# A transformer's first mixer: buffers, batches and order of the convolution's taps on three engines

## The reference

```python
a, gate = split(u)                      # 512 channels each
h = a * sigmoid(gate)
h = depthwise_causal_conv(h, conv_dw)   # 31 taps per channel
h = silu(layer_norm(h + conv_dw_b)) @ w_conv_pw
attn = sliding_window_attention(q, k, v, sinks, rel_bias)   # window 128
x = x + rms_norm(concat(attn, h) @ w_out)
```

## Time and profile before

| | us |
|---|---|
| median of 3 runs | 2300.67 (2300.66 to 2301.5) |
| the profiled execution | 2300.79 |
| its span, first to last instruction | 2299.0 |
| TensorE busy | 2266.1 (99%) |
| VectorE busy | 1358.1 (59%) |
| ScalarE busy | 1037.4 (45%) |
| GpSimd busy | 1028.4 (45%) |
| mean granted TensorE clock | 0.997 of full speed |

### The profile page before, as it was taken

How to read it: one execution, slowest core, us unless ns; L and a number is a source line. 1 busy time by engine, 2 the same in 40 slices (tenths; PEclk the granted TensorE clock), 3 DMA queues, 4 the chain that set the end, 5 groups by cost and what they waited for, 6 DMA issues and landing times.

```text
span 2299.0 us, 30705 instructions
## 1 busy us (share of the span) xinstructions
PE 2266.1 (99%) x11442; PEld 1889.6 (82%) x11442; DVE 1358.1 (59%) x2182; ACT 1037.4 (45%) x2057; POOL 1028.4 (45%) x900
## 2 busy tenths in 40 slices
PE   9989999999999999999999999999999999999998
PEld 7777788888888888888898878887888888888887
DVE  6996516954545477775633775154594444547776
ACT  6577735433232345455634765135443323234543
POOL 2886535488787700032112031224448878770003
PEclk9999999999999999999999999999999999999999
DMA  6122134233233368664002001243223323336865
GB/s 213 37 74 79 51 123 134 73 110 126 85 125 104 113 247 297 213 208 127 20 10 72 24 10 38 76 163 110 101 78 102 126 85 126 103 116 247 295 211 194
DMA packets 218980, 278.48 MB, mean 121 GB/s; under 512 B 16396, under 2 KB 142988, under 8 KB 215760
## 3 DMA queue, kind: packets, MB, share of 16 engines
q1 hardware_dynamic: 199056, 212.81, 29.3%
q10 hardware_dynamic: 19776, 63.71, 7.0%
HBM read 208.30 MB, written 68.17 MB: 120 GB/s over the span
## 4 chain that ended last, share of the span: by engine, by line
PE 87%; POOL 4%; DVE 3%; ACT 3%; issue 1%; DMA 1%; SPq 0%; POOLq 0%; ACTq 0%; DVEq 0%
PE P L513 25%; PE P L515 25%; PE P L514 25%; POOL acc L1315 3%; PE P L3242 3%; PE P L3261 2%; PE P L3277 2%; PE P L3199 1%; PE P L525 1%; ACT wh L473 1%; PE P L1602 1%; DVE P L1242 0%; DVE P L1235 0%; PE P L809 0%; PE P L1627 0%
## 5 line engine op out<-in xcount | busy, mean ns | idle before, releaser
L513 PE MATMUL P<-ah,wh 128*128 128x512 f32 x1120 | 440.6, 393 | 8.4 <-DVE wl L479 4.8
L515 PE MATMUL P<-ah,wl 128*128 128x512 f32 x1120 | 437.6, 391 | 0.0
L514 PE MATMUL P<-al,wh 128*128 128x512 f32 x1120 | 437.1, 390 | 0.0
L513 PE MATMUL P<-wh,ah 128*128 128x512 f32 (+2 forms) x1128 | 425.9, 378 | 0.0
L515 PE MATMUL P<-wh,al 128*128 128x512 f32 (+2 forms) x1128 | 423.3, 375 | 0.0
L514 PE MATMUL P<-wl,ah 128*128 128x512 f32 (+2 forms) x1128 | 422.9, 375 | 0.0
L595 POOL TENSOR_TENSOR stats<-stats,epsc 128x1 f32<-128x1 f32 x70 | 27.7, 396 | 633.0 <-ACT xn L2088 421.0
L513 PEld LDWEIGHTS P<-ah,wh 128*128 128x128 f32 x1120 | 211.3, 189 | 54.6 <-issue 6.9
L515 PEld LDWEIGHTS P<-ah,wl 128*128 128x128 f32 x1120 | 210.9, 188 | 44.3
L514 PEld LDWEIGHTS P<-al,wh 128*128 128x128 f32 x1120 | 211.3, 189 | 43.0
L515 PEld LDWEIGHTS P<-wh,al 128*128 128x128 f32 x1128 | 212.2, 188 | 36.9
(11 more groups left out here) (399 smaller groups left out, 4433.2 us busy)
## 6 DMA issues: line engine op xcount, KB each, us to landing
rf<-ff_rows SPq DMA_DIRECT2D x154, 256.0 KB, 5.3
stage<-in_w_down_dram SPq DMA_DIRECT2D x110, 256.0 KB, 3.8
ff_rows<-sb ACTq DMA_DIRECT2D x22, 1024.0 KB, 5.0
stage<-in_w_gu_dram SPq DMA_DIRECT2D x44, 512.0 KB, 5.1
stage<-in_w_gate_dram SPq DMA_DIRECT2D x22, 512.0 KB, 4.1
stage<-in_w_up_dram SPq DMA_DIRECT2D x22, 512.0 KB, 5.1
ff_rows<-uo ACTq DMA_DIRECT2D x22, 512.0 KB, 3.0
stage<-in_w_down_dram SPq DMA_DIRECT2D x22, 512.0 KB, 5.1
```

What stands on the lines that cost most here:

```text
L513: e.matmul(out, lh, rh, start=start, stop=False, skip_group_check=onto)
L514: e.matmul(out, lh, rl, start=False, stop=False, skip_group_check=onto)
L515: return e.matmul(out, ll, rh, start=False, stop=stop, skip_group_check=onto)
```

## The change

There are now four product places of 512 columns, in the same memory; a half product takes one, a wide one two, and a wide product waits for the addition two before it, the first two wide ones for the last half. VectorE's 19 taps of block 2 end in a tile of their own, `taps_of_2`, where the sigmoid buffers were. ScalarE's product of tap 19 starts `acc` of block 2, the other eleven are added without waiting for VectorE, and a new last addition of GpSimd adds `taps_of_2`. All that waited for the last tap waits for this. The batches of products behind the th = 1 copies have 3 instead of 4. VectorE does 7 of the 14 taps behind `glu(0, 1)` and the lower half of piece 5, and the lower halves of pieces 7 and 9 move ahead of the last 7 taps and of `glu(c, 1)`.

```diff
--- before.py
+++ after.py
@@ -990,7 +990,8 @@
     acc_split = acc[:, :, :].rearrange("p c (two n) -> p c two n", two=2)
     SPLIT = (1, 3)
     tap_sums = sb("tap_sums", [128, 4, 16], off["extra"])
-    tap_products = [sb(f"tap_product{i}", [128, 1024], off["extra"] + 256 + 4 * KB * i) for i in range(2)]
+    taps_of_2 = sb("taps_of_2", [128, 1024], off["sg"])
+    tap_products = sb("tap_products", [128, 4, 512], off["extra"] + 256)
     roots = sb("token_roots", [128, 1024], off["extra"] + 256 + 8 * KB)
 
     def first_piece(port, part, landing, key):
@@ -1224,7 +1225,7 @@
                 ins = e.tensor_scalar(both, hp[:, c, 0:1024], cwt[:, c, 0:1], bias, ALU.mult, ALU.add)
             else:
                 behind("whole")
-                ins = e.scalar_tensor_tensor(acc[:, c, :] if j == SHARED - 1 else both, hp[:, c, j:j + 1024],
+                ins = e.scalar_tensor_tensor(taps_of_2[:, :] if j == SHARED - 1 else both, hp[:, c, j:j + 1024],
                                              cwt[:, c, j:j + 1], both, ALU.mult, ALU.add)
         elif name == "even":
             w = cwt[:, c, 2 * j:2 * j + 1]
@@ -1276,9 +1277,23 @@
 
     PRODUCTS = [(0, a, a + 512, w) for a in (0, 512) for w in range(TAPS)]
     PRODUCTS += [(2, 0, 1024, w) for w in range(SHARED, TAPS)]
-    STARTS = {(0, 0, 0), (0, 512, 0)}
+    STARTS = {(0, 0, 0), (0, 512, 0), (2, 0, SHARED)}
     ADDED = [(c, a, b, w) for c, a, b, w in PRODUCTS if (c, a, w) not in STARTS]
+    HALVES = sum(b - a == 512 for _, a, b, _ in ADDED)
     ADDED_AT = {(c, a, w): k for k, (c, a, b, w) in enumerate(ADDED)}
+
+    def product_place(k):
+
+        c, a, b, w = ADDED[k]
+        if b - a == 512:
+            return tap_products[:, k % 4, :]
+        return tap_products[:, 2 * (k % 2):2 * (k % 2) + 2, :].rearrange("p i n -> p (i n)")
+
+    def place_left(k):
+
+        if k < HALVES:
+            return k - 4
+        return k - 2 if k >= HALVES + 2 else HALVES - 1
 
     def some_products(n):
 
@@ -1291,28 +1306,29 @@
                     AC.wait_ge(ev, ("u", c, th))
                 AC.wait_ge(l_misc, "all")
                 AC.wait_ge(zf, "hp")
-                e.activation(acc[:, c, a:b], src, ACT.Identity, bias=cwt[:, c, 31:32], scale=weight).then_inc(
-                    *ep.up((c, a, w)))
+                if c:
+                    ins = e.activation(acc[:, c, a:b], src, ACT.Copy, scale=weight)
+                else:
+                    ins = e.activation(acc[:, c, a:b], src, ACT.Identity, bias=cwt[:, c, 31:32], scale=weight)
+                ins.then_inc(*ep.up((c, a, w)))
             else:
                 k = ADDED_AT[c, a, w]
                 for th in range(b // 512):
                     AC.wait_ge(ev, ("u", c, th))
-                if k >= 2:
-                    c2, a2, _, w2 = ADDED[k - 2]
+                if place_left(k) >= 0:
+                    c2, a2, _, w2 = ADDED[place_left(k)]
                     AC.wait_ge(pt, (c2, a2, w2))
-                e.activation(tap_products[k % 2][:, 0:b - a], src, ACT.Copy, scale=weight).then_inc(*ep.up((c, a, w)))
+                e.activation(product_place(k), src, ACT.Copy, scale=weight).then_inc(*ep.up((c, a, w)))
             n -= (b - a) / 512
 
     def pool_taps(c):
         for k, (c_, a, b, w) in enumerate(ADDED):
             if c_ == c:
                 PL.wait_ge(ep, (c, a, w))
-                if c:
-                    PL.wait_ge(tap, ("whole", 2, SHARED - 1))
                 if k:
                     c2, a2, _, w2 = ADDED[k - 1]
                     PL.wait_ge(pt, (c2, a2, w2))
-                PL.e.tensor_tensor(acc[:, c, a:b], acc[:, c, a:b], tap_products[k % 2][:, 0:b - a], ALU.add).then_inc(
+                PL.e.tensor_tensor(acc[:, c, a:b], acc[:, c, a:b], product_place(k), ALU.add).then_inc(
                     *pt.up((c, a, w)))
 
     def mixer1_act():
@@ -1391,7 +1407,7 @@
                 kv_copy(name, th)
                 if th == 0:
                     send_to(c + i + 3)
-                some_products(4)
+                some_products(3 if th else 4)
             if name == "q0":
                 for g in range(2):
                     AC.wait_ge(tp, ("v1", g))
@@ -1479,10 +1495,11 @@
         glu(1, 1)
         low_by_dve_to(4)
         add_taps(1)
-        some_taps(14)
+        some_taps(7)
         glu(0, 1)
         low_by_dve_to(5)
         DV.ends("u0")
+        some_taps(7)
         for c in range(2, 4):
             some_taps(9)
             gate(c)
@@ -1490,9 +1507,10 @@
             some_taps(5)
             values(c)
             glu(c, 0)
-            some_taps(12)
+            some_taps(5)
+            low_by_dve_to(2 * c + 3)
+            some_taps(7)
             glu(c, 1)
-            low_by_dve_to(2 * c + 3)
             add_taps(c)
         low_by_dve_to(first["kvq"])
         for i, name in enumerate(KVQ):
@@ -1516,6 +1534,9 @@
         PL.wait_ge(pz, "kp1")
         pool_taps(0)
         pool_taps(2)
+        PL.wait_ge(tap, ("whole", 2, SHARED - 1))
+        PL.wait_ge(pt, (2, 0, TAPS - 1))
+        PL.e.tensor_tensor(acc[:, 2, :], acc[:, 2, :], taps_of_2[:, :], ALU.add).then_inc(*pt.up((2, "whole")))
         PL.ends("q3")
 
 
@@ -1640,7 +1661,7 @@
             b = SWA_BANK["yc", tb]
             claim(b, cp, ("yc", tb))
             for c in range(4):
-                PE.wait_ge(*((tap, ("out", c, 0)) if c in SPLIT else (pt, (2, 0, TAPS - 1))))
+                PE.wait_ge(*((tap, ("out", c, 0)) if c in SPLIT else (pt, (2, "whole"))))
             for c in range(4):
                 ins = e.transpose(P[:, b, 128 * c:128 * c + 128], conv_rows(c, tb), ident[:, :])
             ins.then_inc(*tp.up(("yc", tb)))
@@ -1798,7 +1819,7 @@
             DV.wait_ge(nb, "b1")
             DV.wait_ge(sm, "nsink")
             if i in (2, 3):
-                DV.wait_ge(pt, (2, 0, TAPS - 1))
+                DV.wait_ge(pt, (2, "whole"))
             if i >= 4:
                 DV.wait_ge(tp, ("swa", i - 4))
             elif i < 2:
@@ -1874,7 +1895,7 @@
             PL.e.tensor_tensor(p, p, swa_rows(n)[2][:, 2 * g:2 * g + 2].unsqueeze(2).to_broadcast([128, 2, W]),
                                ALU.mult).then_inc(*nr.up(("swa", i)))
 
-        PL.wait_ge(pt, (2, 0, TAPS - 1))
+        PL.wait_ge(pt, (2, "whole"))
         for i in range(2):
             sink_column(i)
         for i in range(N1 + 4):
```

## The result

The changed kernel takes **2306.03 us** (median of 11 runs, 2305.65 to 2306.99) against 2300.78 for the kernel before (11 runs): a ratio of 1.0023, 95% interval 1.0015 to 1.0031. It is slower by 5.2 us. The profiled execution took 2306.6, with a span of 2304.8 against 2299.0, 5.8 more.

The account below looks back on a forecast made before the run. GpSimd's last addition was taken to set the start of attention. 2300.79 less 0.4 for its earlier end plus 1.9 for TensorE's slow clock gave 2302.3 for the profiled run, 2302.2 for the median; range 2298.0 to 2305.5.

Parts of the forecast that it names:

- the new waits at 143 to 157: GpSimd's waits for products late in the convolution, forecast at 1 to 2 us each.
- +1.9 forecast: At the start of attention: TensorE's clock falls after a longer idle, costing 2.4 less 0.5 of later slack.
- Last addition: 146.5 + 32.0 + 2.5 = 181.0: GpSimd's third block: first wide addition at 146.5, twelve taking 32.0, waits 2.5; the end 0.4 earlier than 181.40.
- Bounds: the same lower half took 1.23 and 1.70 ..., about 2 us, either way: Uncertainty from lower halves lengthening beside GpSimd's additions: half of some ten times 0.47 in the stage, about 2 us.
- VectorE is 0.8 later at the sigmoid of block 2: After the moved taps VectorE waits 1.7 for TensorE, to 57.6, and everything behind that sigmoid is 0.8 later too.
- that gives the 0.8 back and VectorE is level from 95.85: At piece 8 VectorE waits 1.65 instead of 2.65 because ScalarE is no longer late, recovering the 0.8.
- gains of 3.0 and 0.2: GpSimd: 3.0 from its next addition coming at 121.1, 0.2 from no longer waiting for VectorE's last tap.
- 1.5, 1.2 and 1.1: GpSimd's new waits: 1.5 at the last half product, 1.2 at the first wide product, and 1.1 more.
- C: Rival, 13%: TensorE's clock stays low through the first attention steps, 183.3 to 195, losing 5.5; time 2305.0.
- D: Rival, 22%: the clock does not fall in the idle ahead of attention, or added waits just balance; time 2300.3.
- B: Rival, 12%: GpSimd keeps ahead without new waits, VectorE's queue is next; 4.6 at most, 2296.1, likelier half 2298.4.
- A: Rival, 3%: TensorE bounds the first stage, so its stalls count in full, 11.3 us; time 2289.4.

Follow-up runs that it names:

- e10: Changed kernel with the lower half of piece 14 made three taps earlier, while GpSimd waits: 2302.95 us, ratio 1.0010.
- e15: Kernel before with the lower half of piece 14 made three taps later, beside wide additions: 2304.49 us, ratio 1.0014.
- e1: Changed kernel with VectorE doing 14 taps again, not 7, ahead of the second product of block 0: 2303.57 us, ratio 1.0011.
- e14: Changed kernel with 14 taps again ahead of the product of block 0 and piece 14's lower half three taps earlier: 2300.64 us, ratio 0.9997.
- e5: Kernel before with only the four product places and the rule for them: 2298.05 us, ratio 0.9987.
- e12: Kernel before with the four product places and ScalarE's copies of v ahead of its copies of q0: 2299.67 us, ratio 0.9995.
- e2: Changed kernel with batches of 4 products again behind every copy, not 3 behind the upper-token ones: 2306.42 us, ratio 1.0021.
- e6: Changed kernel with both 14 taps ahead of the product of block 0 and batches of 4 again: 2303.18 us, ratio 1.0009.
- e7: Kernel before with only the own place for VectorE's third-block taps, tap 19 starting ScalarE's sum, and GpSimd's last addition: 2302.19 us, ratio 1.0007.
- e8: Kernel before with only the lower halves of pieces 7 and 9 made 7 taps earlier: 2303.37 us, ratio 1.0012.

## Why the prediction was wrong

**Right.** GpSimd's last addition set the start of attention, in both kernels: the first transposes follow it by 2.26 and 2.27. The removed stalls of TensorE were worth nothing. VectorE waits at 57 (2.17; forecast 1.7), GpSimd's wait near 122 is 1.77 (1.3), the new waits at 143 to 157 are there. TensorE's clock fell, at +1.9 forecast and 1.5 to 2.3 measured. With GpSimd's end put right (3.8 later in place of 0.4 earlier) the forecast's own sum gives 2306.5 for the profiled execution, which took 2306.6. That closeness is partly chance, as the clock's term is known to 0.8 only.

**Wrong.** The failed step is "Last addition: 146.5 + 32.0 + 2.5 = 181.0", with its term "Bounds: the same lower half took 1.23 and 1.70 ..., about 2 us, either way". I kept each lower half at its old length at its new place. It depends on what GpSimd does at that moment: e10 shows 1.21 against 3.41 for the same piece, e15 3.01 against 1.21. GpSimd ended at 185.19, 4.2 later than forecast: the first wide addition was 2.05 late (148.55 for 146.5), and the wait ahead of 171.97 was 2.70, not 0.5. That wait is piece 14 and the sum of rows ahead of it, 3.4 longer on VectorE; e10 takes it away and GpSimd ends 3.1 earlier. The upper end of the range fell short by 0.5 us.

The lateness of the first wide addition comes from the step before: "VectorE is 0.8 later at the sigmoid of block 2" and "that gives the 0.8 back and VectorE is level from 95.85". It was 1.57 late at 72.93 and still 1.51 late at 97.36. The moved taps were given their wait for TensorE (2.17 for 1.7), but not the 0.83 by which piece 5 is longer at its new place, and piece 7 takes 0.80 more as well. e1 undoes the wait and piece 5 and is worth 3.0 at GpSimd's end. With both undone (e14) the end is 6.1 earlier and the time is that of the kernel before. The two terms come to more than the 3.8 by which the changed kernel is late, because its other parts, the four places above all, gain.

Two sums in the prediction do not hold as written, without weight for the result. The "gains of 3.0 and 0.2" less "1.5, 1.2 and 1.1" are 0.6 later, not 0.4 earlier; what is missing is the wait of 1.16 that the old kernel had ahead of GpSimd's run at 131.47, and which the longer run of 14 halves removes. And the estimate from the Trainium skill's 426.7 and 215.7 ns ("TensorE: Matmul & The Clock Gate", Wait — 56ns, not 53.3ns?) is 2.5, not 2.6: ten times 0.211, and 0.4 for the transposes. The trace's own spacings, 0.43 and 0.227, are near it.

Of the rivals, C came out with the right sign and near the right time by a reason that was not the one: the slow clock cost 1.5 to 2.3, not 5.5, and the rest was GpSimd's end. D is refuted by the granted clock of 0.50 in 184 to 192. B is what four places do without the change's other parts: e5 has it, at 2298.05 (B's likelier half: 2298.4), though there TensorE comes last and not VectorE, so the agreement is luck. A, TensorE as the bound, is refuted by the changed kernel, where TensorE reached the scores 2.1 earlier (177.79 for 179.91) and the end came later, and by e12, where it reached them 9 us earlier than in e5 and nothing was gained (VectorE's last conversion was 2.9 later there).

The Trainium skill ("SBUF — State Buffer", Who interferes with whom) says that a VectorE instruction with two SBUF inputs contends with a GpSimd instruction that reads SBUF, and calls the port pair that they share an exclusive lock. As an estimate from that rule and the rows here, a lower half that comes just behind the start of a wide addition (2.4) waits for up to all of it and takes up to about 3.6 with its own 1.2. The trace agrees: the longest single lower halves beside wide additions took 3.01 to 3.43, others there 1.67 to 2.45, and the taps, with one input in PSUM, kept their 0.75. What the runs show by themselves is that the length hangs on GpSimd's work beside it; that the port is the reason is the Trainium skill's. The bound that I should have used is, for every such operation, one whole addition.

Left open: the split of e2's lost gain between piece 13 and the order of products was not tried by itself, nor was the changed kernel without the place of its own for VectorE's taps. Nor was e5 with its copies of v moved only behind the q0 products, which might shorten TensorE's 7.0 without making VectorE wait.

## What to carry to other kernels

An instruction's length can belong to its place and not to the instruction. Here a VectorE operation with both inputs in SBUF took 1.21 alone and up to 3.43 beside GpSimd's wide additions: for every such operation that a change shifts, price it with and without the whole GpSimd instruction that may lie ahead of it, and let it move all that follows. Test a change of several edits one edit at a time, since here the one useful edit (four places, 2.8 faster) was hidden under the others. Before two profiles are set against each other, look whether they agree ahead of the edit: e1's began 1.57 late, which hid half of its gain. And an engine that is made to arrive early is not free: TensorE's idle time ahead of attention cost 1.5 to 2.3 us of clock.

## What was not expected of the hardware

One lower half moved by three taps, some 2 us, changed the whole kernel by 3.1 us down (e10) or 3.6 up (e15), without any change in the amount of work. Each time the cost is on both sides: the additions beside a lower half took up to 3.20 for 2.41. The granted clock was low behind an idle of 3.05 to 3.25 too (e6, e7), and behind 1.68 in e15, while with 1.17 and 1.18 (e8, the kernel before) it stayed at 1.00. In e7 it fell only behind the idle time: 1.00 in 182 to 184, 0.81 in 184 to 186, when TensorE was at work again from 184.17, and 0.50 in 186 to 188.
